# Who copies the small block of turned probabilities: ScalarE ahead of its large copy, in place of VectorE behind the group norm

## The chip, the cores and the metric

The kernel runs on one core of a Trainium2 chip. The metric is the device time of one execution in microseconds. The engines of the core work side by side and wait for each other on semaphores: TensorE (PE) multiplies, VectorE (DVE) and ScalarE (ACT) read and write both memories, GpSimd (POOL) works in SBUF, and SyncE (SP) issues the transfers. Each engine takes its own instructions in the order in which they are written.

## The reference

One layer of a streaming encoder over 256 tokens of width 2048, in fp32:

```
h = RMSNorm(x);  p = h @ w_in
r = Retention(p[ret cols])           # 8 heads of 128: (q k^T * decay) v, group norm, swish gate
s = SlidingWindowGQA(p[swa cols])    # 16 query heads of 64, 2 kv heads, window 128 = 2 chunks, learned sinks
x = x + concat([r, s]) @ w_out
x = x + (gelu(conv3(a)) * b) @ w_ffn_out,  a, b = split(RMSNorm(x) @ w_ffn_in)
y = RMSNorm(x)
```

What the change touches is the attention part s: for every query head the softmax p of the scores over the window, and o = p v. Query tokens 0 to 127 see 128 keys, tokens 128 to 255 see 192 keys (64 to 255).

## The kernel before, in words

All weights (about 200 MB) are streamed once. A weight tile of 128x1024 elements lands in one of eight slots of raw (SyncE, waiting until the slot's old tile is used up), ScalarE writes its rounded high half into w_hi (line 728, the function hi), VectorE the rest into w_lo (line 977, lo), and TensorE forms each product of three passes (lines 414 to 416). There are four slots of w_hi and w_lo, so hi and lo work four tiles ahead of TensorE.

The stretch that matters is that of the eight heads (s = 0 to 7): six in a loop with two per turn, the last two written out. While TensorE computes the projection of the next retention head in eight weight tiles (k = 0 to 7, product(k)), the attention of head s is woven in between the tiles. TensorE's order is in its attention_step: the scores of a pair of attention heads, then behind tile 1 the turned q and k (qk_turn), behind tile 2 the retention scores, behind tile 3 the retention values (ret_values, lines 551 to 553), behind tile 4 the turned probabilities (probs_turn), behind tile 6 the attention values (swa_values, lines 569 to 573), behind tile 7 the turned output (mix_turn, line 580). probs_turn leaves six blocks in PSUM: four of 128x128 in bank_s0, and two of 64x128 (the last 64 keys) in bank_s1. They have to be copied to SBUF, as p_t (128x512) and p_t2 (64x256), before swa_values can read them. swa_values waits for p_t_ready, p_t2_ready and ret_p_ready, and in half of the loop's heads for shift_landed.

ScalarE's order in a head: high half of tile 5 (split(5)), probs_out (p_t, line 801), high half of tile 6, which waits until TensorE has used a tile, high half of tile 7, and then the copies of the projection and of the outputs. VectorE's order: statistics of the group norm, low half of tile 4, the rest of the group norm (lines 1150 to 1157, an inverse root in many small steps), low half of tile 5, probs_out (p_t2, line 1139), low half of tile 6, low half of tile 7, mix_out. GpSimd multiplies the normed output with its gate (mix_tok, line 1356), which mix_turn waits for.

The order of the instructions is written by hand; there is no planner.

Of the kernel before, what the change touches and what calls it, by code (L numbers as in the profile page):

```python
# [27 lines left out]
ACT = mybir.ActivationFunctionType  # L28
AX_X = mybir.AxisListType.X

P = 128
# [73 lines left out]
def build(nc, x, ln1, w_in, b_swa, ret_gn, sinks, w_out, ln2, w_ffn_in, conv_w, conv_b, w_ffn_out,  # L105
# [10 lines left out]
    with ExitStack() as ctx:  # L116
# [3 lines left out]
        def sem(name):  # L120
            return ctx.enter_context(nc.semaphore(name))
# [18 lines left out]
        def s1(name, shape, dt=F32):  # L140
            return sb(name, shape, dt, part1)
# [34 lines left out]
        p_t2 = s1("p_t2", [P, 2, P])  # L176
# [28 lines left out]
        bank_s0, bank_s1, bank_t, bank_r = bank_s[:, 0, :], bank_s[:, 1, :], bank_tr[:, 0, :], bank_tr[:, 1, :]  # L205
# [47 lines left out]
        probs_turned = sem("probs_turned")  # L253
        p_t_ready = sem("p_t_ready")
        p_t2_ready = sem("p_t2_ready")
# [462 lines left out]
        def _(act):  # L718
            run = nc.scalar.activation
# [78 lines left out]

            def probs_out(s):
                act.wait_ge(probs_turned, s + 1)  # L800
                run(p_t[:], bank_s0[:].rearrange("p (a b n) -> p a b n", a=2, b=2), ACT.Copy).then_inc(p_t_ready, 1)

            def mix_out(s, pair):
# [8 lines left out]
            def attention_step(s, j, pair, split, last):  # L812
                split(0)
                tanh_gate(s, j)
                split(1)
                qk_out(s)
                exp_scores(s)
                split(2)
                split(3)
                norm_probs(s)  # L820
                split(4)
                split(5)
                probs_out(s)
                split(6)
                split(7)
                if not last:
                    act.wait_ge(ret_done, s + 1)
                    to_sbuf(1 - j, s * 8 + (HEAD_TILE + 15), head_in_sbuf)
                mix_out(s, pair)
# [139 lines left out]
        def _(dve):  # L969
# [119 lines left out]
            def mask_scores(s):  # L1089
                dve.wait_ge(scores_done, s + 1)  # L1090
                for a, bank in enumerate((bank_s0, bank_s1)):
                    tt(probs[:, a, :], bank[:, 0:P + KEYS1], mask[:], ALU.add).then_inc(masked, 1)

            def score_max(s, pair):

                dve.wait_ge(masked, s * 2 + 2)
                for b, keys in enumerate((slice(0, P), slice(P, P + KEYS1))):
                    nc.vector.reduce_max(row_max[:, 2 * b:2 * b + 2], probs[:, :, keys], AX_X).then_inc(row_max_ready, 1)
                sinks2 = neg_sink[:, bass.ds(pair * 2, 2)].unsqueeze(1).broadcast_to([P, TOK, 2])
                dve.wait_ge(row_max_ready, s * 2 + 2)  # L1100
                stt(out=neg_max[:].rearrange("p (b a) -> p b a", b=TOK),
                    in0=row_max[:].rearrange("p (b a) -> p b a", b=TOK), scalar=-1.0, in1=sinks2,
                    op0=ALU.mult, op1=ALU.min).then_inc(neg_max_ready, 1)
                dve.wait_ge(neg_max_ready, s + 1)
                tt(sink_in[:].rearrange("p (b a) -> p b a", b=TOK),
                   neg_max[:].rearrange("p (b a) -> p b a", b=TOK), sinks2, ALU.subtract).then_inc(sink_in_ready, 1)

            def rotate(s, j):

                dve.wait_ge(head_in_sbuf, s * TOK + TOK)  # L1110
                tt(rot_a[:], proj[:, j, :, 0:2, :],
                   rope[:, :, 0:1, :].broadcast_to([P, TOK, 2, P]), ALU.mult).then_inc(rot_a_ready, 1)
                dve.wait_ge(rot_a_ready, s + 1)
                dve.wait_ge(rot_b_ready, s * 4 + 4)
                tt(qk_rot[:], rot_a[:], rot_b[:], ALU.add).then_inc(rot_ready, 1)

            def swish(s, j):

                dve.wait_ge(gate_t_ready, s + 1)
                stt(out=gate[:], in0=gate_t[:], scalar=1.0, in1=proj[:, j, :, 3, :],  # L1120
                    op0=ALU.add, op1=ALU.mult).then_inc(gate_ready, 1)

            def denominators(s):
                dve.wait_ge(probs_ready, s * 5 + 5)
                tt(denom[:], p_sum[:], sink_e[:], ALU.add).then_inc(denom_ready, 1)
                dve.wait_ge(denom_ready, s + 1)
                nc.vector.reciprocal(r_denom[:], denom[:]).then_inc(r_denom_ready, 1)

            def decay_scores(s):

                dve.wait_ge(ret_scores_done, s + 1)
                tt(ret_p[:, 0:2 * P].unsqueeze(1), bank_r[:, 0:2 * P].unsqueeze(1), decay[:, bass.ds(s, 1), :],
                   ALU.mult).then_inc(ret_p_ready, 1)
                tt(ret_p[:, 2 * P:3 * P].unsqueeze(1), bank_r[:, 2 * P:3 * P].unsqueeze(1),
                   decay[:, bass.ds(s, 1), 0:P], ALU.mult).then_inc(ret_p_ready, 1)

            def probs_out(s):
                dve.wait_ge(probs_turned, s + 1)
                nc.vector.tensor_copy(p_t2[0:64, :, :],
                                      bank_s1[0:64, 0:2 * P].rearrange("p (a n) -> p a n", a=2)).then_inc(p_t2_ready, 1)  # L1140

            def group_norm(s, split):

                dve.wait_ge(ret_done, s + 1)
                for t in range(TOK):
                    nc.vector.bn_stats(o_stats[:, t, :], bank_t[:, t * P:(t + 1) * P]).then_inc(o_stats_ready, 1)
                dve.wait_ge(o_stats_ready, s * 2 + 2)
                split(4)
                for t in range(TOK):
                    nc.vector.bn_aggr(o_mv[:, t, :], o_stats[:, t, :]).then_inc(o_mv_ready, 1)  # L1150
                dve.wait_ge(o_mv_ready, s * 2 + 2)
                ts(o_var[:], o_mv[:, :, 1], EPS, None, ALU.add).then_inc(o_var_ready, 1)
                dve.wait_ge(o_var_ready, s + 1)
                inverse_root(s + 1, o_var[:], o_rstd[:], o_rstd_ready)
                dve.wait_ge(o_rstd_ready, s + 1)
                for t in range(TOK):
                    ts(o_norm[:, t, :], bank_t[:, t * P:(t + 1) * P], o_mv[:, t, 0:1], o_rstd[:, t:t + 1],
                       ALU.subtract, ALU.mult).then_inc(o_norm_ready, 1)

            def mix_out(s, pair):  # L1160

                dve.wait_ge(mix_hi_ready, s * 2 + 2)
                own, other = bass.ds(s, 1), bass.ds(pair + RET_HEADS, 1)
                stt(out=mix_lo[:, own, :], in0=bank_r[:, 0:SEQ].unsqueeze(1), scalar=cols[:, bass.ds(s + C_GN, 1)],
                    in1=mix_hi[:, own, :].bitcast(F32), op0=ALU.mult, op1=ALU.subtract).then_inc(mix_lo_ready, 1)
                tt(mix_lo[:, other, :], bank_r[:, SEQ:2 * SEQ].unsqueeze(1), mix_hi[:, other, :].bitcast(F32),
                   ALU.subtract).then_inc(mix_lo_ready, 1)

            def attention_step(s, j, pair, split):
                rotate(s, j)  # L1170
                mask_scores(s)
                score_max(s, pair)
                split(0)
                swish(s, j)
                split(1)
                split(2)
                decay_scores(s)
                denominators(s)
                split(3)
                group_norm(s, split)  # L1180
                split(5)
                probs_out(s)
                split(6)
                split(7)
                mix_out(s, pair)

            ahead = HEAD_TILE + 8 + SPLIT
            with dve.Fori(0, RET_HEADS // 2 - 1) as i:
                for j in range(2):
                    attention_step(i * 2 + j, j, i + 4 * j, lambda k: lo(ahead + 8 * j + k, i, 16))  # L1190
            for s in (RET_HEADS - 2, RET_HEADS - 1):
                attention_step(s, s % 2, s // 2 + 4 * (s % 2), lambda k: lo(ahead + 8 * s + k))
# [245 lines left out]
```

## Time and profile before

| | |
|---|---|
| median of 3 runs | 1135.54 us (1134.43 to 1137.92) |
| profiled execution | 1136.41 us, its span on the core 1134.6 us |
| mean granted TensorE clock | 0.992 |
| PE / DVE / ACT / POOL busy | 1106.1 / 695.7 / 563.1 / 75.3 us |
| DMA | 206.80 MB, mean 182 GB/s |

Times in the rows are microseconds from the start of the span, unless marked ns. PE is the matmul, PEld the weight load that overlaps it. A busy time of PE is not PE at its peak, since ends of matmuls are modelled and consecutive ones overlap. Brackets name the idle time ahead of an instruction and who ended it.

### The profile page before, as it was taken

The numbers are of one execution on the slowest core, as the hardware profiler recorded it, in microseconds if no ns is written. First come the engines' busy times: TensorE is split into PE (matmuls) and PEld (weight loads), VectorE is DVE, ScalarE is ACT, GpSimd is POOL, SyncE is SP. The second block draws the span as 40 slices with busy tenths as digits, with TensorE's granted clock in tenths as the row PEclk, the third lists the DMA queues.
The fourth block names the chain that finished last, engine by engine and source line by source line (L and its number), as shares of the span: only waits on it lengthen the run. The fifth ranks groups of instructions, "written<-read, shape, count | busy, mean of one in ns | idle before, by whom it ended". The sixth has DMA issues, their size and how long they took to land.

```text
span 1134.6 us, 16771 instructions
## 1 busy us (share of the span) xinstructions
PE 1106.1 (97%) x5746; PEld 936.7 (83%) x5746; DVE 695.7 (61%) x1002; ACT 563.1 (50%) x792; POOL 75.3 (7%) x86
## 2 busy tenths in 40 slices
PE   7999999999999999999999999999999899999996
PEld 6888777777778888888888888888888788888885
DVE  4655666666656575656656657556566555575555
ACT  5545555555545445544545545445455454454443
POOL 2000111111100001101101001011011000000001
PEclk8999999999999999999999999999999999999998
DMA  9766555554556666666666666666666556556641
GB/s 340 235 188 175 149 151 154 156 150 148 149 173 180 186 184 187 188 187 191 190 187 185 187 186 189 190 191 185 186 186 193 189 195 195 189 186 202 197 135 74
DMA packets 146240, 206.80 MB, mean 182 GB/s; under 512 B 7539, under 2 KB 75537, under 8 KB 145952
## 3 DMA queue, kind: packets, MB, share of 16 engines
q1 hardware_dynamic: 145632, 204.67, 59.7%
q0 software_dynamic: 544, 1.72, 0.4%
q8 instruction: 18, 0.29, 0.1%
q14 instruction: 14, 0.11, 0.0%
q10 hardware_dynamic: 32, 0.01, 0.0%
HBM read 204.17 MB, written 2.10 MB: 182 GB/s over the span
## 4 chain that ended last, share of the span: by engine, by line
PE 96%; DVE 1%; DMA 1%; issue 1%; ACT 0%; SPq 0%; DVEq 0%; ACTq 0%
PE acc L634 14%; PE acc L414 13%; PE acc L416 13%; PE acc L415 13%; PE acc L640 7%; PE bank_s L634 7%; PE bank_tr L634 7%; PE bank_tr L640 4%; PE bank_s L640 4%; PE bank_s L416 2%; PE bank_s L415 2%; PE bank_s L414 2%; PE bank_tr L416 2%; PE bank_tr L414 2%; PE bank_tr L415 2%; DMA raw<-in_w_in 1%
## 5 line engine op out<-in xcount | busy, mean ns | idle before, releaser
L977 DVE TENSOR_TENSOR w_lo<-raw,w_hi 128x1024 fp32r<-128x1024 f32 x380 | 465.5, 1226 | 405.7 <-ACT w_hi L728 403.5
L728 ACT ACTIVATE w_hi<-raw 128x1024 fp32r<-128x1024 f32 x380 | 403.0, 1061 | 553.0 <-PE acc L416 178.5
L634 PE MATMUL acc<-h_both,w_hi 128*128 128x512 f32 x704 | 220.3, 394 | 0.0
L414 PE MATMUL acc<-w_hi,h_both 128*128 128x512 f32 (+1 forms) x352 | 139.2, 395 | 1.9 <-DVE h_both L984 1.9
L640 PE MATMUL acc<-h_both,w_lo 128*128 128x256 f32 x704 | 140.6, 282 | 0.0
L416 PE MATMUL acc<-w_hi,h_both 128*128 128x512 f32 (+1 forms) x352 | 134.6, 382 | 0.0
L415 PE MATMUL acc<-w_lo,h_both 128*128 128x512 f32 (+1 forms) x352 | 134.4, 382 | 0.0
L634 PEld LDWEIGHTS acc<-h_both,w_hi 128*128 128x128 f32 x704 | 121.1, 190 | 15.1
L640 PEld LDWEIGHTS acc<-h_both,w_lo 128*128 128x128 f32 x704 | 121.0, 190 | 13.7
L634 PE MATMUL bank_s<-h_both,w_hi 128*128 128x512 f32 x352 | 109.0, 391 | 0.0
L634 PE MATMUL bank_tr<-h_both,w_hi 128*128 128x512 f32 x352 | 109.0, 390 | 0.0
L414 PEld LDWEIGHTS acc<-w_hi,h_both 128*128 128x128 f32 x352 | 66.9, 190 | 16.4 <-issue 2.8
L634 PEld LDWEIGHTS bank_tr<-h_both,w_hi 128*128 128x128 f32 x352 | 66.1, 188 | 15.1
L634 PEld LDWEIGHTS bank_s<-h_both,w_hi 128*128 128x128 f32 x352 | 66.1, 188 | 15.1
L416 PEld LDWEIGHTS acc<-w_hi,h_both 128*128 128x128 f32 x352 | 66.7, 190 | 13.2
L415 PEld LDWEIGHTS acc<-w_lo,h_both 128*128 128x128 f32 x352 | 67.0, 190 | 11.2
L414 PE MATMUL acc<-w_hi,g_hi 128*128 128x512 f32 x176 | 68.9, 392 | 3.2 <-DVE g_lo L1250 3.2
L640 PE MATMUL bank_tr<-h_both,w_lo 128*128 128x256 f32 x352 | 70.9, 283 | 0.0
L640 PE MATMUL bank_s<-h_both,w_lo 128*128 128x256 f32 x352 | 70.9, 283 | 0.0
L1386 POOL TENSOR_TENSOR conv<-conv,rstd_row 128x512 f32<-128x512 f32 x22 | 33.9, 1540 | 528.9 <-ACT conv L883 528.9
L415 PE MATMUL acc<-w_lo,g_hi 128*128 128x512 f32 x176 | 68.7, 390 | 0.0
L416 PE MATMUL acc<-w_hi,g_lo 128*128 128x512 f32 x176 | 68.7, 390 | 0.0
(168 smaller groups left out, 1341.2 us busy)
## 6 DMA issues: line engine op xcount, KB each, us to landing
raw<-in_w_ffn_in SPq DMA_DIRECT2D x176, 512.0 KB, 3.6
raw<-in_w_ffn_out SPq DMA_DIRECT2D x88, 512.0 KB, 3.8
raw<-in_w_in SPq DMA_DIRECT2D x128, 256.0 KB, 3.1
raw<-in_w_out SPq DMA_DIRECT2D x32, 512.0 KB, 3.8
raw<-in_w_in SPq DMA_DIRECT2D x20, 512.0 KB, 8.4
x_res<-in_x SPq DMA_DIRECT2D x4, 512.0 KB, 10.2
decay<-table_decay POOLq DMA_DIRECT2D x1, 1024.0 KB, 9.4
lnf_row<-in_ln_f SPq DMA_DIRECT2D x1, 1024.0 KB, 7.3
```

The costliest lines, as they stand in the source:

```text
L414: mm(out, lhs_hi, rhs_hi, start=first, stop=False, skip_group_check=True)
L415: mm(out, lhs_hi, rhs_lo, start=False, stop=False, skip_group_check=True)
L416: return mm(out, lhs_lo, rhs_hi, start=False, stop=last, skip_group_check=True)
L634: mm(out, w_hi[:, slot, q * COLS + ft * P:q * COLS + (ft + 1) * P], h_both[:, 2 * k + q, :, :].rearrange("p a n -> p (a n)"), start=k == 0 ...
L640: ins = mm(out, w_lo[:, slot, q * COLS + ft * P:q * COLS + (ft + 1) * P], h_hi[:, 2 * k + q, :], start=False, stop=k == 7 and q == 1, skip ...
L728: run(w_hi[:, n % SPLIT, :], raw[:, n % RAW, :], ACT.Copy).then_inc(hi_ready, 1)
L977: tt(w_lo[:, n % SPLIT, :], raw[:, n % RAW, :], w_hi[:, n % SPLIT, :].bitcast(F32), ALU.subtract).then_inc(lo_ready, 1)
L1386: nc.gpsimd.tensor_tensor(conv[:, own, :], conv[:, own, :], rstd_row[:].unsqueeze(1).broadcast_to([P, 2, SEQ]), ALU.mult).then_inc(gate_re ...
```

## The change

The copy of p_t2 moves from VectorE to ScalarE. On ScalarE it stands in probs_out, behind the same wait for probs_turned and ahead of the copy of p_t. On VectorE probs_out is gone, so that the low halves of tiles 5 and 6 follow each other. TensorE's instructions and waits are the same; p_t2_ready is now raised by ScalarE.

```diff
             def probs_out(s):
                 act.wait_ge(probs_turned, s + 1)
+                run(p_t2[0:64, :, :], bank_s1[0:64, 0:2 * P].rearrange("p (a n) -> p a n", a=2),
+                    ACT.Copy).then_inc(p_t2_ready, 1)
                 run(p_t[:], bank_s0[:].rearrange("p (a b n) -> p a b n", a=2, b=2), ACT.Copy).then_inc(p_t_ready, 1)
...
-            def probs_out(s):
-                dve.wait_ge(probs_turned, s + 1)
-                nc.vector.tensor_copy(p_t2[0:64, :, :],
-                                      bank_s1[0:64, 0:2 * P].rearrange("p (a n) -> p a n", a=2)).then_inc(p_t2_ready, 1)
-
...
                 split(3)
                 group_norm(s, split)
                 split(5)
-                probs_out(s)
                 split(6)
                 split(7)
                 mix_out(s, pair)
```

## Rows read from the trace of the kernel before

**Rows 1.** The page's busy table: busy us, share of the span, instructions.

```profile
PE 1106.1 (97%) x5746; PEld 936.7 (83%) x5746; DVE 695.7 (61%) x1002; ACT 563.1 (50%) x792; POOL 75.3 (7%) x86
```

**Rows 2.** Busy time of each engine in the stretch of the eight heads.

```profile
core 0: us, PE busy (x) PEld busy (x) DVE busy (x) ACT busy (x) POOL busy (x), PEclk, DMA share, GB/s
97.00:320.00 223.00, 215.06 (x1109) 173.11 (x1108) 146.43 (x335) 115.69 (x223) 32.03 (x47) 1.00 0.52 153
```

**Rows 3.** List of waits, whole span: who waited <- for whom: total us, times, longest.

```profile
ACT w_hi L728 <- PE acc L416: 178.5, 103, 4.0
...
PEld bank_tr L569 <- issue: 11.1, 8, 1.5
ACT w_hi L728 <- DMA raw<-in_w_in: 10.5, 2, 5.4
PE bank_tr L569 <- issue: 7.9, 8, 1.1
```

**Rows 4.** Timeline around swa_values, second head: start, us, engine, line, operation [idle before].

```profile
145.03 1.06 ACT L728 ACTIVATE w_hi<-raw 128x1024 fp32r<-128x1024 f32 x1 [2.35 <-PE acc L416]
146.00 0.58 ACT L801 ACTIVATE p_t<-bank_s 128x512 f32<-128x512 f32 x1
146.50 0.73 DVE L1157 TENSOR_SCALAR o_norm<-bank_tr,o_mv,o_rstd 128x128 f32<-128x128 f32 x2
147.15 1.22 DVE L977 TENSOR_TENSOR w_lo<-raw,w_hi 128x1024 fp32r<-128x1024 f32 x1
147.32 0.39 PE L416 MATMUL acc<-w_hi,h_both 128*128 128x512 f32 x1
147.38 1.57 POOL L1356 TENSOR_TENSOR mix_tok<-gate,o_norm 128x256 f32<-128x256 f32 x1 [17.63 <-DVE o_norm L1157]
147.75 1.06 ACT L728 ACTIVATE w_hi<-raw 128x1024 fp32r<-128x1024 f32 x1 [1.18 <-PE acc L416]
148.28 0.41 DVE L1139 COPY p_t<-bank_s 64x256 f32<-64x256 f32 x1
148.76 0.23 PEld L569 LDWEIGHTS bank_tr<-p_t,kv_tok 128*64 128x64 f32 x4 [1.48 <-issue]
148.79 0.44 PE L569 MATMUL bank_tr<-p_t,kv_tok 128*64 128x128 f32 x4 [1.08 <-issue]
148.84 1.23 DVE L977 TENSOR_TENSOR w_lo<-raw,w_hi 128x1024 fp32r<-128x1024 f32 x1
```

**Rows 5.** Timeline around swa_values in the first head.

```profile
118.25 0.58 ACT L801 ACTIVATE p_t<-bank_s 128x512 f32<-128x512 f32 x1
119.57 0.39 PE L416 MATMUL acc<-w_hi,h_both 128*128 128x512 f32 x1
120.39 0.41 DVE L1139 COPY p_t<-bank_s 64x256 f32<-64x256 f32 x1
120.87 0.23 PEld L569 LDWEIGHTS bank_tr<-p_t,kv_tok 128*64 128x64 f32 x4 [1.34 <-issue]
120.90 0.44 PE L569 MATMUL bank_tr<-p_t,kv_tok 128*64 128x128 f32 x4 [0.94 <-issue]
```

**Rows 6.** Timeline of the second head where ret_values follow product tile 3.

```profile
137.76 0.39 PE L416 MATMUL acc<-w_hi,h_both 128*128 128x512 f32 x1
137.76 0.41 PEld L551 LDWEIGHTS bank_tr<-proj,ret_p 128*128 128x128 f32 x2
137.99 0.38 PE L551 MATMUL bank_tr<-proj,ret_p 128*128 128x128 f32 x2
```

**Rows 7.** Timeline of TensorE around swa_values in the last head.

```profile
313.99 0.39 PE L416 MATMUL acc<-w_hi,mix_lo 128*128 128x512 f32 x1
315.45 0.44 PE L569 MATMUL bank_tr<-p_t,kv_tok 128*64 128x128 f32 x4 [1.07 <-issue]
```

**Rows 8.** Timeline of the end of the second head and the start of the third.

```profile
152.38 0.37 PEld L580 LDWEIGHTS bank_tr<-ident,mix_tok 128*128 128x128 f32 x2
152.81 1.06 ACT L728 ACTIVATE w_hi<-raw 128x1024 fp32r<-128x1024 f32 x1 [4.00 <-PE acc L416]
152.92 0.52 PEld L520 LDWEIGHTS bank_s<-k_heads,q_now 64*128 64x128 f32 x8 [0.17 <-issue]
153.77 1.25 ACT L743 ACTIVATE proj<-acc,rstd 128x512 f32<-128x512 f32 x2
```

**Rows 9.** Durations by line, ns min/median/max, first and last start, forms.

```profile
L809 ACT ACTIVATE mix_hi<-bank_tr x8: 375/392/392, 127.4 to 320.9; 128x256 f32 x6, 128x256 fp32r<-128x256 f32 x2
L1139 DVE COPY p_t<-bank_s x8: 406/407/411, 120.4 to 314.9; 64x256 f32<-64x256 f32 x8
```

**Rows 10.** DMA issues: engine, operation, count, KB each, median us from issue to landing.

```profile
raw<-in_w_in SPq DMA_DIRECT2D x128, 256.0 KB, 3.1
```

## The prediction

> **What bounds the kernel now.** I read the page's busy table first. TensorE is busy for 97% of the span, VectorE for 61% and ScalarE for 50% [rows 1]. So a moved copy of 0.4 us counts only if TensorE waits for it. The next view is the busy time of the stretch of the eight heads, 97 to 320 us. It holds 223.0 us, of which TensorE is busy 215.06, at a granted clock of 1.00 [rows 2]. It sits idle there for 7.9 us. The list of waits puts this idle time in one place: 7.9 us, 8 times, in front of line 569, the first matmul of swa_values [rows 3]. That is one stall of about 1 us per head. The list calls its releaser "issue", so the true releaser has to be read from the order of time. The rest of TensorE's time goes to matmuls in a row, and ScalarE waits for it (178.5 us in front of the rounding of weights) [rows 3]. That makes TensorE the bound, and time taken from its stall is time taken from the kernel, unless a later wait takes it back.
>
> The second head's timeline shows who releases it [rows 4]. The last matmul of tile 6 starts at 147.32. ScalarE has finished p_t (146.00 + 0.58 = 146.58) before that. VectorE is still on its group norm: o_norm from 146.50, the low half of a weight tile from 147.15, and only then the small copy (line 1139), from 148.28 to 148.69. The weight load of line 569 starts at 148.76, 0.07 us after the copy's end. The first head repeats the pattern: the copy ends at 120.39 + 0.41 = 120.80 and the weight load starts at 120.87 [rows 5]. Twice the same 0.07 us makes p_t2_ready the wait that ends last. ret_p was there when line 551 read it at 137.99 [rows 6], and p_t 2.2 us before.
>
> **The change part by part.**
>
> *The stall that goes.* What would TensorE do without it? Line 551 of the same head also follows a product tile, and its wait is met in time. Its weight load starts together with the last product matmul (137.76), and its first matmul starts 0.23 us after it (137.99) [rows 6]. With the stall, the same distance is 148.79 - 147.32 = 1.47 us in the second head, 120.90 - 119.57 = 1.33 in the first and 315.45 - 313.99 = 1.46 in the last [rows 4, 5, 7]. Over the eight heads there are five distances of 1.33 or 1.34 and three of 1.46 or 1.47, 11.05 us together. Without the stall they would be 8 x 0.23 = 1.84. The difference is 9.2 us. Check: the idle time is counted from the modelled end of the last matmul, 0.39 after its start, so it misses 0.16 us per head: 7.9 + 8 x 0.16 = 9.2. I take 9.2. Bounds: at the most the weight loads' idle time, 11.1 us [rows 3]. At the least, a small bubble stays: in front of line 520, where small matmuls follow small matmuls, 0.17 us of "issue" remains [rows 8]. Swa_values waits on three or four semaphores, so it could keep as much, 8 x 0.17 = 1.4, which leaves 7.8.
>
> *The copy that ScalarE gets.* The nearest row in engine, source (PSUM) and 256 columns is line 809 at 392 ns [rows 9]. It has 128 partitions in place of 64. The copy on VectorE, 64x256, took 407 ns in this trace [rows 9]. Consecutive ScalarE instructions overlap: line 728 at 145.03 takes 1.06 us, and line 801 starts at 146.00, 0.09 before its end [rows 4]. So p_t moves later by 0.39 - 0.09 = 0.30 us. The bounds are 0 (if the copy hid completely) and 0.97, the start distance of the rounding of a whole weight tile, four times as wide [rows 4]. I take 0.30. The chain for p_t in the second head is then: small copy 146.00 to 146.39, large copy 146.30 to 146.88, release at about 146.95 with the same 0.07. The weight load that I expect at 147.33 has 0.38 us left over. In the first head the large copy starts at 118.25 and TensorE could go on from 119.57 [rows 5]: 118.25 + 0.30 + 0.58 + 0.07 = 119.20, so 0.37 is left. The copy costs nothing as long as it adds less than 0.67 us.
>
> The Trainium skill ("ScalarE: Activation LUTs", Rules for kernel authors) speaks against moving such work: it says to give relu, max, add and mul to VectorE and not to ScalarE, since VectorE is faster per element, up to three times in bf16. For fp32 out of PSUM the rows don't bear this out (392 against 407 ns); were the copy three times as long on ScalarE, 1.22 us, p_t would be about 0.46 us late and the gain would be 5.5 us, not 9.2. By this the kernel still ends faster.
>
> *What stands behind the copy on ScalarE.* The next instruction is the rounding of tile 6 at 147.75, and it waits until then for TensorE, 1.18 us idle [rows 4]. The 0.30 us vanish in that gap. No DMA and no other queue is passed: ScalarE issues no transfer in the heads.
>
> *What VectorE loses.* 8 x 0.41 = 3.3 us of work. The low half of tile 6 can't start earlier than at 148.84 in the second head, since it needs the high half, 147.75 + 1.06 = 148.81 [rows 4]. So VectorE does nothing sooner, and the buffer releases that start the weight transfers move only where TensorE itself moves. Price 0.
>
> *What is late next.* Behind the stall everything on TensorE comes some 1.15 us earlier. Mix_turn then stands at 152.38 - 1.24 = 151.14. It needs mix_tok, which GpSimd has finished at 147.38 + 1.57 = 148.95 [rows 4, 8], a margin of 2.2 us. The rounding of tile 7 has 4.00 us of idle time in front of it, all spent waiting for TensorE [rows 8], so ScalarE follows and about 2.8 us remain. It is also the point where each head is lined up with TensorE anew: to_sbuf, rotary and scores of the next head are counted from there, and move as a whole. Weights: ScalarE waited for a transfer of w_in twice in the whole kernel [rows 3], the median landing took 3.1 us [rows 10], and the DMA engines are 52% busy in the heads [rows 2]. The eight-slot ring has room for 1.2 us in 28. Nothing takes the gain back.
>
> *The sum.* The profiled execution took 1136.41 us, with a span of 1134.6 and 1.8 around it; less 9.2 is 1127.2. The median of the three runs is 1135.54, 0.9 below, and the stall has nothing that hangs on the profiler: 1135.54 - 9.2 = 1126.3 us.
>
> **The rivals.**
>
> *The large copy takes the small one's place.* If the ScalarE copy adds more than 0.67 us, TensorE waits for p_t. At the upper bound 0.97 it would be 0.30 late in each head: 9.2 - 8 x 0.30 = 6.8 gained, 1128.7 us. Against it: 392 ns in the nearest row. Chance 0.06.
>
> *No change.* Either the wait named "issue" is not the copy's but another one's (the loop's branch, ret_p, the shift transfer), or a later wait of the same head eats the gain: 1135.5 us. Against the first: 0.07 us behind the copy, twice, and the stall is there in the last two heads too, which stand outside the loop. Against the second: the margin of 2.2 us at mix_turn. For it: TensorE waits on up to four semaphores there, and the profile gives only the order of time. Chance 0.07.
>
> *Slower: the copy in front blocks ScalarE's queue.* ScalarE works in order, so all that the small copy adds beyond cover is passed on to p_t, and behind it to the rounding of tile 6. The cover is 0.67 us up to TensorE's earliest start; from there another 1.15 us only uses up the removed stall. The change becomes a loss from 1.8 us added per head, and a loss of over 0.3% (3.4 us, 0.43 per head) from about 2.25. The price at 2.25 is 1139 us. Two 128x512 copies with a scale take 1.25 us together [rows 8], so nothing in this trace of this size comes near. Chance 0.02.
>
> **How the numbers follow.** The forecast itself, 1126.3, has 0.85. Its own bounds are a gain of 7.8 to 11.1 us, or 1124.4 to 1127.7. The median of a few runs adds some: the three runs of before lie between 1.1 below and 2.4 above their median. That gives 1123.3 to 1130.1. The first rival lies inside at 1128.7, and with the runs' spread it asks for 1131. So the range is 1123.3 to 1131.0, and it leaves out the no-change case and the slower one, 0.09, and some of the tails. A measurement of this kernel can tell about 0.3%, 3.4 us, from no change. Faster by more: forecast and first rival, 0.91. Within: 0.07. Slower: 0.02.
>
> **What would show it.** Right: in the heads' stretch TensorE's idle time falls from 7.9 us to under 1.5, and the wait in front of line 569 (its number will move) goes. The distance from the last product matmul to it becomes 0.23 us. ScalarE shows two copies with 0.30 us between their starts, the small one about 0.39 long. The rounding of tile 6 still waits for TensorE, now about 0.9 us, and the head period, 27.8 us, shortens by 1.15. Wrong: a distance between 0.3 and 1.3 us with ScalarE's large copy 0.07 us before the weight load (first rival), an unchanged distance, or new idle time at mix_turn or in front of the next product tile. The size would be off if the twelve small matmuls of swa_values run more slowly once TensorE reaches them without a pause.

## The result and the profile after

The changed kernel takes 1126.79 us (median of 5 runs, 1124.22 to 1129.54). The kernel before takes 1135.20 (1134.43 to 1137.92, 5 runs). The ratio is 0.9928, with a 95% interval of 0.9908 to 0.9947, so 8.4 us or 0.7% faster. The prediction was 1126.3.

The profiled execution took 1127.33 us with a span of 1125.5. The busy table of its page:

```profile
PE 1105.9 (98%) x5746; PEld 936.6 (83%) x5746; DVE 693.5 (62%) x994; ACT 565.3 (50%) x800; POOL 75.2 (7%) x86
```

The stretch of the eight heads, busy time by engine (columns as in [rows 2]):

```profile
97.00:320.00 223.00, 223.00 (x1145) 179.94 (x1142) 148.39 (x332) 121.91 (x236) 32.04 (x47) 1.00 0.54 158
```

VectorE runs 8 instructions fewer and ScalarE 8 more. TensorE is now "busy" for all of the 223.00 us of the stretch, where [rows 2] had 215.06. The list of waits of the changed kernel, the lines of the heads' attention:

```profile
ACT w_hi L728 <- PE acc L416: 168.0, 103, 2.9
...
PEld bank_tr L569 <- issue: 2.8, 8, 0.4
...
PEld bank_s L520 <- issue: 1.5, 8, 0.4
...
PEld bank_tr L573 <- issue: 1.4, 8, 0.2
```

The line "PE bank_tr L569 <- issue: 7.9" of [rows 3] is gone. The one for its weight load has fallen from 11.1 to 2.8 us and not to nothing. ScalarE's longest wait for TensorE fell from 4.0 to 2.9 us, since TensorE comes sooner.

The timeline of the second head of the changed kernel, to be laid beside [rows 4] and, from 149.50 on, [rows 8]:

```profile
144.25 0.36 ACT L801 ACTIVATE p_t<-bank_s 64x256 f32<-64x256 f32 x1
...
144.51 0.58 ACT L803 ACTIVATE p_t<-bank_s 128x512 f32<-128x512 f32 x1
...
145.53 1.22 DVE L979 TENSOR_TENSOR w_lo<-raw,w_hi 128x1024 fp32r<-128x1024 f32 x1
145.57 0.39 PE L416 MATMUL acc<-w_hi,h_both 128*128 128x512 f32 x1
145.76 1.58 POOL L1352 TENSOR_TENSOR mix_tok<-gate,o_norm 128x256 f32<-128x256 f32 x1 [17.77 <-DVE o_norm L1154]
145.89 0.20 PEld L569 LDWEIGHTS bank_tr<-p_t,kv_tok 128*64 128x64 f32 x4 [0.35 <-issue]
145.89 0.44 PE L569 MATMUL bank_tr<-p_t,kv_tok 128*64 128x128 f32 x4
146.00 1.06 ACT L728 ACTIVATE w_hi<-raw 128x1024 fp32r<-128x1024 f32 x1 [0.91 <-PE acc L416]
...
147.09 1.34 DVE L979 TENSOR_TENSOR w_lo<-raw,w_hi 128x1024 fp32r<-128x1024 f32 x1 [0.34 <-ACT w_hi L728]
...
149.50 0.37 PEld L580 LDWEIGHTS bank_tr<-ident,mix_tok 128*128 128x128 f32 x2
...
149.92 1.06 ACT L728 ACTIVATE w_hi<-raw 128x1024 fp32r<-128x1024 f32 x1 [2.87 <-PE acc L416]
```

Both copies are done at 145.09, and the matmul of line 569 starts at 145.89, 0.32 us behind the last product matmul. In [rows 4] it was 1.47. All eight heads read 0.32. The time of the eight heads can be measured without their surroundings by the way from line 569 of the first head to line 569 of the last: 315.45 - 120.90 = 194.55 us before [rows 5, 7], and 187.18 after, from these rows of the first and the last head:

```profile
119.15 0.44 PE L569 MATMUL bank_tr<-p_t,kv_tok 128*64 128x128 f32 x4
...
306.33 0.44 PE L569 MATMUL bank_tr<-p_t,kv_tok 128*64 128x128 f32 x4
```

This is 7.37 us for seven heads, 1.05 for one, 8.4 for eight. From the last head to the end of the span it is 819.15 us before and 819.17 after: nothing is given back. The spans differ by 9.1 and not by 8.4 because the start-up stage in front of the first head's stall was 0.74 us shorter in this execution (last product matmul at 118.83, before at 119.57). That is chance: in the profiles of the runs below, whose start-up is the same or nearly so, that last product matmul comes anywhere between 117.13 and 119.53.

### The profile page after: what moved, and what is told of

Read it like the earlier page. It is cut to its first block, busy times and chain, and to the rows that moved or that the text cites. A ratio compares the mean times of both kernels' runs of the same rounds, so it can differ in the third digit from the quotient of the medians.

```text
span 1125.5 us, 16771 instructions
## 1 busy us (share of the span) xinstructions
PE 1105.9 (98%) x5746; PEld 936.6 (83%) x5746; DVE 693.5 (62%) x994; ACT 565.3 (50%) x800; POOL 75.2 (7%) x86
## 4 chain that ended last, share of the span: by engine, by line
PE 97%; DVE 1%; DMA 1%; ACT 0%; SPq 0%; issue 0%; DVEq 0%; ACTq 0%
PE acc L634 14%; PE acc L414 13%; PE acc L416 13%; PE acc L415 13%; PE acc L640 7%; PE bank_s L634 7%; PE bank_tr L634 7%; PE bank_tr L640 4%; PE bank_s L640 4%; PE bank_s L416 2%; PE bank_s L414 2%; PE bank_s L415 2%; PE bank_tr L416 2%; PE bank_tr L414 2%; PE bank_tr L415 2%; DMA raw<-in_w_in 1%
```

## The experiments

The theory: TensorE waited for p_t2 only because its copy stood behind the group norm and the low half of tile 5 in VectorE's queue. The rivals: VectorE's lighter load, the engine itself, the order of the two copies. Seven heads means the way from line 569 (or its like) in the first head to the last, as above. It is the sharp measure, since it repeats to 0.01 us (187.18 in both profiles of the changed kernel), while single runs of one kernel differ by some 5 us.

**VectorE keeps a copy at the old place.** The changed kernel, with

```diff
+            def probs_out(s):
+                dve.wait_ge(probs_turned, s + 1)
+                nc.vector.tensor_copy(p_spare[0:64, :, :],
+                                      bank_t[0:64, 0:2 * P].rearrange("p (a n) -> p a n", a=2))
...
                 split(5)
+                probs_out(s)
                 split(6)
```

> The changed kernel, and VectorE also copies a 64x256 block of PSUM (from bank_t, into a spare tile that nobody reads) at the old place, behind the low half of tile 5. Theory (TensorE waited for the place of the copy in VectorE's queue, not for VectorE's load): VectorE does the 3.3 us of before again, nobody waits for it, the time is that of the changed kernel, about 8.4 us under before (1126 to 1128), and the matmuls of line 569 start 0.32 us behind the last product matmul. Rival (VectorE's lighter load made the gain): the time is that of before, 1134 to 1136.

Measured: 1126.10 us, ratio to before 0.9919 (0.9893 to 0.9945), seven heads 187.18 us. In the trace the spare copy stands at its old place and TensorE passes it by:

```profile
145.31 0.44 PE L570 MATMUL bank_tr<-p_t,kv_tok 128*64 128x128 f32 x4
...
145.95 0.41 DVE L1142 COPY p_spare<-bank_tr 64x256 f32<-64x256 f32 x1
```

So the 3.3 us of VectorE's work were worth nothing. The rival falls.

**VectorE's copy one place earlier.** The kernel before, with

```diff
                 group_norm(s, split)
+                probs_out(s)
                 split(5)
-                probs_out(s)
                 split(6)
```

> The kernel before, with VectorE's copy one place earlier, ahead of the low half of tile 5. Theory (place in the queue): the copy starts where the low half started, 147.15 in the second head of before, ends at 147.56 and releases TensorE at about 147.63, 0.31 us behind the last product matmul, which is where the changed kernel's line 569 starts anyway (0.32). So the time is that of the changed kernel, about 8 us under before, though ScalarE does nothing more. Rival (it has to be ScalarE, since VectorE is the busier engine): as before, 1134 to 1136.

Measured: 1126.50 us, ratio 0.9929 (0.9903 to 0.9955), seven heads 187.19 us. The timeline of its second head:

```profile
143.69 0.41 DVE L1139 COPY p_t<-bank_s 64x256 f32<-64x256 f32 x1
...
144.18 0.21 PEld L569 LDWEIGHTS bank_tr<-p_t,kv_tok 128*64 128x64 f32 x4 [0.35 <-issue]
144.20 0.44 PE L569 MATMUL bank_tr<-p_t,kv_tok 128*64 128x128 f32 x4
```

The copy ends at 144.10 and TensorE starts 0.33 us behind its last product matmul (143.87): just in time. Two lines exchanged on VectorE bring what the change to ScalarE brings.

**VectorE's copy three places earlier.** The kernel before, with the copy behind the low half of tile 4:

```diff
                 split(4)
+                probs_out(s)
                 for t in range(TOK):
                     nc.vector.bn_aggr(o_mv[:, t, :], o_stats[:, t, :]).then_inc(o_mv_ready, 1)
...
                 split(5)
-                probs_out(s)
                 split(6)
```

> The kernel before, with VectorE's copy three places earlier, right behind the low half of tile 4 and ahead of the rest of the group norm. Theory: the copy ends at about 144.3 in the second head, three microseconds ahead of TensorE; the group norm comes 0.41 us later, and mix_tok with it, where 2.2 us are left at mix_turn. Time as the changed kernel, about 8.4 us under before. Rival (the later group norm becomes the new wait at mix_turn): a new wait in front of line 580, and less gain.

Measured: 1127.38 us, ratio 0.9936 (0.9916 to 0.9956), seven heads 187.18 us. Mix_tok is later against TensorE's line 569 than in the changed kernel (0.13 us behind its start, where the changed kernel has it 0.13 ahead), and ends with 1.9 us to spare:

```profile
145.31 1.58 POOL L1356 TENSOR_TENSOR mix_tok<-gate,o_norm 128x256 f32<-128x256 f32 x1 [18.03 <-DVE o_norm L1158]
...
148.78 0.37 PEld L580 LDWEIGHTS bank_tr<-ident,mix_tok 128*128 128x128 f32 x2
```

The group norm has room for the 0.41 us. No new wait appeared.

**The large copy first.** The changed kernel, with

```diff
+                run(p_t[:], bank_s0[:].rearrange("p (a b n) -> p a b n", a=2, b=2), ACT.Copy).then_inc(p_t_ready, 1)
                 run(p_t2[0:64, :, :], bank_s1[0:64, 0:2 * P].rearrange("p (a n) -> p a n", a=2),
                     ACT.Copy).then_inc(p_t2_ready, 1)
-                run(p_t[:], bank_s0[:].rearrange("p (a b n) -> p a b n", a=2, b=2), ACT.Copy).then_inc(p_t_ready, 1)
```

> The changed kernel with ScalarE's two copies in the other order, the large one first. Theory (both copies are done before TensorE wants them): no change against the changed kernel, line 569 starts 0.32 us behind the last product matmul; the second copy ends near 145.1 in the second head of the changed kernel, as before the swap. Rival (the order matters, since what TensorE needs first is p_t): the distance and with it the time get smaller by up to 0.09 us per head, 0.7 us together.

Measured: 1126.93 us, ratio 0.9931 (0.9906 to 0.9956), seven heads 187.18 us. "In front of the large copy" is of no weight.

**Two spare copies ahead of the large one.** The changed kernel, with

```diff
+                for spare in (rot_a[:], qk_t[:].rearrange("p a (b n) -> p a b n", b=2)):
+                    run(spare, bank_s0[:].rearrange("p (a b n) -> p a b n", a=2, b=2), ACT.Copy)
                 run(p_t[:], bank_s0[:].rearrange("p (a b n) -> p a b n", a=2, b=2), ACT.Copy).then_inc(p_t_ready, 1)
```

> The changed kernel with two spare 128x512 copies by ScalarE between the small and the large one (0.48 us each by start distance, 0.97 together; they write tiles that nobody reads by then). Theory (cover of ScalarE's queue): in the second head of the changed kernel the large copy ended at 145.09 and line 569's weight load began at 145.89; with 0.97 more it ends at 146.06 and releases at 146.13, 0.24 us late in each head, so 1.9 us slower than the changed kernel, still some 6.5 under before. Rival (ScalarE's queue is no limit, or the whole delay is passed on): no change, or 8 x 0.97 = 7.8 us slower than the changed kernel.

Measured: 1129.20 us, ratio 0.9948 (0.9932 to 0.9965), seven heads 188.78 us. That is 1.60 us over the changed kernel, 0.23 a head, 1.8 for eight. The large copy now ends last, and the list of waits names it:

```profile
PEld bank_tr L569 <- ACT p_t L805: 4.6, 8, 0.6
```

**Four spare copies.** The same with rot_a, rot_b, qk_t and a spare tile.

```diff
+                for spare in (rot_a[:], rot_b[:], qk_t[:].rearrange("p a (b n) -> p a b n", b=2), p_spare[:]):
+                    run(spare, bank_s0[:].rearrange("p (a b n) -> p a b n", a=2, b=2), ACT.Copy)
```

> The changed kernel with four spare 128x512 copies by ScalarE ahead of the large one, 1.94 us together. Theory: the large copy ends 1.94 us later, 1.2 us behind what TensorE could use, in each of eight heads: 9.7 us slower than the changed kernel, 1136 to 1138, so about 1 us slower than before. This is the place from which the slower rival of the prediction decides. Rival (later places give some of it back, or ScalarE's late rounding of tile 6 adds its own wait): clearly under 1134, or over 1140.

Measured: 1135.80 us, ratio to before 1.0008 (0.9997 to 1.0019), seven heads 195.32 us, 1.16 a head over the changed kernel, 9.3 for eight. The trace of its second head:

```profile
148.05 0.59 ACT L806 ACTIVATE p_t<-bank_s 128x512 f32<-128x512 f32 x1
148.69 0.20 PEld L570 LDWEIGHTS bank_tr<-p_t,kv_tok 128*64 128x64 f32 x4 [1.52 <-ACT p_t L806]
148.69 0.44 PE L570 MATMUL bank_tr<-p_t,kv_tok 128*64 128x128 f32 x4 [1.10 <-ACT p_t L806]
```

The stall is back, with another name: 1.49 us between the last product matmul and line 570 (line 569 of before) in the first head, 1.55 in the last, a little more than the 1.33 to 1.47 of before. That agrees with seven heads that take 0.77 us more than the 194.55 of before. By the trace the four spare copies delay the large one by 1.91 us, not the 1.94 that were expected: it starts at 148.05, the first spare one at 146.14. So ScalarE's queue has room for some 0.7 us beyond its small copy, and from there each microsecond is paid eight times (1.91 - 0.73 = 1.18 against the measured 1.16 a head). At 1.91 us more the whole gain is spent, and 0.1 us a head besides.

**One wait in front of swa_values.** What is left in front of line 569, 0.35 us of the weight load's time, is not in the prediction's sum. Is it the price of its three or four waits? The changed kernel, with

```diff
-                    ACT.Copy).then_inc(p_t2_ready, 1)
+                    ACT.Copy).then_inc(p_t_ready, 1)
...
-                pe.wait_ge(p_t_ready, s + 1)
-                pe.wait_ge(p_t2_ready, s + 1)
-                pe.wait_ge(ret_p_ready, s * 2 + 2)
-                if isinstance(s, int) or j == 0:
-                    pe.wait_ge(shift_landed, 3 * 16)
+                pe.wait_ge(p_t_ready, s * 2 + 2)
...
             pe.wait_ge(k_ready, 2)
+            pe.wait_ge(shift_landed, 3 * 16)
```

> The changed kernel, with one semaphore wait in front of swa_values in place of three or four: both copies raise the same semaphore, and the waits for ret_p_ready and shift_landed are dropped or done once ahead of the loop. In the changed kernel line 569 starts 0.32 us behind the last product matmul and not 0.23, with 0.35 us of idle time in front of its weight load. Theory W (each wait costs TensorE some time): the idle time in front of the weight load falls to nothing and the distance to 0.23. Theory G (a weight load of another size, 64 columns or 64 rows, can't be pulled ahead of a running 128x128 matmul): both stay as they are, 0.35 and 0.32.

Measured: one run, 1127.87 us; seven heads 187.18 us. The idle time didn't move at all (its lines 565 and 569 are lines 569 and 573 of the others):

```profile
PEld bank_tr L565 <- issue: 2.8, 8, 0.4
...
PEld bank_tr L569 <- issue: 1.4, 8, 0.2
```

The two or three waits that were taken away, all met in time, had cost TensorE nothing that can be seen here. Theory W falls. That Theory G is right doesn't follow from this run: it had forecast no more than that nothing would change.

**The last values matmul over 128 rows.** The changed kernel, with

```diff
-                    ins = mm(head(a, 1), v_shift[0:64, 1, kv], p_t2[0:64, a, :], start=False, stop=True,
+                    ins = mm(head(a, 1), v_shift[:, 1, kv], p_t2[:, a, :], start=False, stop=True,
...
             nc.vector.memset(zeros, 0.0).then_inc(zeros_ready, 1)
+            nc.vector.memset(p_t2[64:128, :, :], 0.0)
+            nc.vector.memset(v_shift[64:128, 1, :], 0.0)
```

> The changed kernel, with the last values matmul (line 573) over 128 rows in place of 64: the upper 64 rows of p_t2 and of the shifted values are zeroed once by VectorE at the start. So line 573 has the same size as line 571 in front of it, 128 rows and 64 columns, and no other wait changes. Theory G (a change of size makes the bubble): the idle time of 0.17 us in front of line 573's weight load (8 times, 1.4 us together) goes, that in front of line 569 (0.35) stays, and line 573 starts some 0.1 us sooner behind line 571. Rival (the bubble in front of line 573 comes from something else, as the source tile): it stays at 0.17.

Measured: one run, 1126.03 us; seven heads 186.11 us. The wait in front of line 573 has left the list, that of line 569 is still 2.8. TensorE around it, in the second head, of the changed kernel:

```profile
146.16 0.39 PE L571 MATMUL bank_tr<-p_t,v_shift 128*64 128x128 f32 x4
146.47 0.20 PEld L573 LDWEIGHTS bank_tr<-p_t,v_shift 64*64 64x64 f32 x4 [0.17 <-issue]
146.48 0.44 PE L573 MATMUL bank_tr<-p_t,v_shift 64*64 64x128 f32 x4
```

and of the kernel with 128 rows:

```profile
145.91 0.39 PE L571 MATMUL bank_tr<-p_t,v_shift 128*64 128x128 f32 x4
146.02 0.25 PEld L573 LDWEIGHTS bank_tr<-p_t,v_shift 128*64 128x64 f32 x4
146.13 0.39 PE L573 MATMUL bank_tr<-p_t,v_shift 128*64 128x128 f32 x4
```

The group with a star in a row (128*64) is the piece of the array that the instruction uses, rows by columns. Where it stays 128*64, the first weight load of line 573 starts 0.11 us behind line 571 and not 0.31; the rows of a line are merged, so the starts of the lines (0.22 against 0.32 apart) tell more. Twice as many rows, and 0.10 us sooner. Theory G holds for line 573. As a rule for every change of size it doesn't hold: line 545 changes the size without any idle time (shown in the last section).

**Both timed side by side.** The changed kernel and the one with 128 rows, five runs of each on one chip.

> The changed kernel once more, on the same chip as the next run. Expected 8.4 us under before, 1126 to 1128; the way through seven heads (line 569 of the first to line 569 of the last) 187.2 us.

> The kernel with line 573 over 128 rows, timed beside the changed kernel. The single profile showed the way through seven heads shorter by 1.07 us, 0.15 us a head. Theory G: 186.1 us for the seven heads again, and a median some 1.2 us below that of the changed kernel, which is inside the spread of single runs. Rival (the single profile was chance, or the two memsets at the start cost as much): 187.2 us for the seven heads, or the same median.

Measured: the changed kernel 1125.67 us, ratio to before 0.9924 (0.9911 to 0.9938), seven heads 187.18; with 128 rows 1124.32 us, ratio 0.9909 (0.9896 to 0.9923), seven heads 186.11. By the heads that is 0.15 us each, 1.2 for eight; by the medians 1.35 of 1125.67, but the intervals overlap, so only the trace shows it clear of chance. It is the fastest kernel of this study, 9.7 us under before by the medians.

## Why the prediction was right, point by point

*The bound and the releaser.* Right. That TensorE waited for the copy was read from 0.07 us between the end of the copy and the weight load, twice, though the list said "issue". With the copy elsewhere, in four places on two engines (ahead of and behind ScalarE's large copy, one and three places earlier on VectorE), the stall went each time.

*The stall that goes.* The mechanism was right and the size 0.7 us too large. The sum set 0.23 us as the distance that stays, from line 551, and got 9.2. Measured is 0.32: 11.05 - 8 x 0.32 = 8.5, which agrees with 8.4 by the seven heads and 8.4 by the medians. The mis-sized term is the bubble: I put it at 0 and kept 0.17 a head as the bound. It is 0.09 a head by the matmuls. It was a poor choice of row. Line 551 uses the whole array like the product, while lines 520 and 569 work for two attention heads on two halves of it. The better row was in the trace of before: the first line 520 stands right behind a product tile, and it is the longest of the waits "PEld bank_s L520 <- issue: 1.5, 8, 0.4":

```profile
96.97 0.39 PE L416 MATMUL acc<-w_hi,h_both 128*128 128x512 f32 x1
97.28 0.41 PEld L520 LDWEIGHTS bank_s<-k_heads,q_now 64*128 64x128 f32 x6 [0.35 <-issue]
97.28 0.49 PE L520 MATMUL bank_s<-k_heads,q_now 64*128 64x128 f32 x4
```

The distance is 0.31 us there, and with it the sum would have been 11.05 - 8 x 0.31 = 8.6. The prediction read the 0.17 us of a later line 520 instead, which follows small matmuls [rows 8]. The bound was right and the reason given for it (several waits) wrong, as the run with one wait showed.

*The copy on ScalarE.* Taken at 0.39 us and 0.30 by start distance, measured 0.36 and 0.26. VectorE took 0.41 for the same copy. The rule that the prediction took from the Trainium skill, "ScalarE: Activation LUTs" (Rules for kernel authors), names relu, max, min, add and mul and gives its factor for bf16. For this fp32 copy out of PSUM it isn't borne out; and the two kernels with the copy on VectorE show that the choice of engine made no difference of either sign.

*What stands behind it.* The idle time in front of tile 6's rounding was forecast at 0.9 and is 0.91, at tile 7 forecast 2.8, is 2.87.

*VectorE.* The low half of tile 6 still starts when its high half is done (147.09 against 146.00 + 1.06), and the run with the copy kept showed that its load is worth nothing.

*What is late next.* The margin at mix_turn was forecast at 2.2 us; mix_tok ends at 147.34 and the weight load of line 580 starts at 149.50, so 2.16. Nothing behind the heads takes anything back: 819.15 against 819.17 us. Nor do the weights: ScalarE's waits for transfers of w_in come to 10.5 us before and 10.6 after.

*The rivals.* No change is out: the run with the two lines exchanged moved nothing but VectorE's copy, and the stall went, so no other wait held it; and no later wait ate the gain. The first rival (large copy late) had a distance between 0.3 and 1.3 us as its sign. The 0.32 lies in it, but the sign's other half is missing: the large copy ends 0.80 us before the weight load, not 0.07. It and the slower rival needed a much dearer copy, and the spare copies gave their prices. The prediction let the small copy add 0.67 us before TensorE waits, and 1.82 before the gain is gone. In the changed kernel the copy adds 0.26, and 145.89 - 0.07 - 145.09 = 0.73 are left over, 0.99 together. With the gain of 1.05 a head that makes 2.04 to the point of no gain. The four spare copies lie 0.13 beyond it (0.26 + 1.91 = 2.17) and were 0.11 us a head slower than before. The first threshold came out 0.32 too low, because line 569's weight load starts 0.32 us behind the last product matmul and not 0.01. The second is the first plus the gain of a head; that gain came out 0.10 less than forecast, which leaves it 0.22 too low.

*The size by the spans.* The two profiled spans differ by 9.1 us, near to my 9.2, but that is luck: 0.74 of it comes from the start-up.

## What to carry to other kernels

A short copy that TensorE waits for is to be placed by when its input is there and when its reader wants it, not by the engine's load: one line earlier on the same engine did as much as moving it to another. Measure a change inside a loop by the distance between two like instructions of the first and last turn; here it repeated to 0.01 us where whole runs spread by several. Before taking "no stall" as zero, look for a place in the trace where the same kind of matmul follows the same neighbour without a wait.

## What the runs showed of the hardware that I had not expected

Some weight loads stand idle for the same time in every head, and the profile of the kernel before names nothing that they wait for. Behind a product tile, the load of line 551 starts together with the last matmul ([rows 6]). Line 569 idles 0.35 us there, and so does the first line 520. Line 573 behind line 571 idles 0.17 us, line 520 behind line 580 0.17, and the next product tile 0.17 behind line 573 and 0.23 behind line 520. In the one case where a run made a pair alike (line 573 over 128 rows, like line 571), its idle time went, and 0.15 us a head with it: 0.10 in front of line 573, and 0.05 between line 573 and the product tile behind it (0.37 us between their starts, then 0.32).

It is not the size of the load by itself. Line 545 loads 128*64 between two loads of 128*128, and neither its load nor the one behind it idles, here in the changed kernel:

```profile
139.78 0.27 PE L544 MATMUL bank_s<-ident,probs 128*128 128x128 f32 x1
139.78 0.11 PEld L545 LDWEIGHTS bank_s<-ident,probs 128*64 128x64 f32 x1
139.88 0.27 PE L545 MATMUL bank_s<-ident,probs 128*64 128x128 f32 x1
139.89 0.14 PEld L543 LDWEIGHTS bank_s<-ident,probs 128*128 128x128 f32 x1
```

What sets lines 520, 569, 571 and 573 apart from it is that they serve two attention heads on two halves of the array: the first two matmuls of line 569 in the second head start at 145.890 and 145.896 us, where those of lines 544 and 545 start 0.11 us apart. Each place with idle time lies at the start or the end of such a group, or where its rows change. That is read from the rows. No run tested it for line 569, so the cause of its 0.35 us stays open.

The Trainium skill ("TensorE: Matmul & The Clock Gate", Step-by-step) says that loads are pulled ahead where row groups don't conflict or the background buffer is their target. The trace agrees for lines 551 and 545, whose loads start together with the matmul in front; why those of lines 520, 569 and 573 don't, no run here shows.

The busy time of TensorE hides this. Its row read 223.00 of 223.00 us in the changed kernel and in the one with 128 rows alike, though the second is 0.15 us a head faster, because a matmul is shown as 0.39 us long while the next starts after 0.23. The Trainium skill ("Trainium Kernel Development and Optimization", Performance Expectations) warns of that row; the weight loads' waits (2.8, 1.5 and 1.4 us) showed what was left.

The profiles differ outside the heads. Line 569 of the first head was at 119.15 us in one profile of the changed kernel and at 119.59 in another, at 117.44 in the one with VectorE's copy moved by a place; the rest behind the last head took 819.17 and 820.23 us in the two profiles of the changed kernel. What varies in the start-up was not looked into.
